# Second strips of three output projections by seven block products, with x spilled and reloaded around them

## The reference, cut to what matters

```
x = x + rmsnorm(mix, g[1])                 # mix   = [mixer result, 256 x 2048] @ w_out (2048 x 2048)
h = rmsnorm(x, g[2])
x = x + rmsnorm(cross_attention, g[3])     # ends in o @ wo (2048 x 2048)
h = rmsnorm(x, g[4])
x = x + rmsnorm(swiglu, g[5])
```

## Time and profile before

| what | us |
|---|---|
| median of 3 runs | 2858.02 (2857.41 to 2858.25) |
| span of the profiled execution | 2856.5 |
| TensorE busy | 2838.7 (99%) |
| VectorE busy | 2120.0 (74%) |
| ScalarE busy | 1546.4 (54%) |
| GpSimd busy | 49.2 (2%) |
| DMA | 582.54 MB, mean 204 GB/s |

### The profile page before, as it was taken

One profiled execution on the slowest core, in us unless ns is written; L12 is line 12 of the kernel. 1 busy time (PEld: TensorE's weight loads), 2 busy tenths in 40 slices (PEclk: granted clock), 3 DMA queues, 4 the chain that ended last, 5 costly groups with the idle time before them and its releaser, 6 DMA issues.

```text
span 2856.5 us, 31752 instructions
## 1 busy us (share of the span) xinstructions
PE 2838.7 (99%) x13038; PEld 2358.0 (83%) x13038; DVE 2120.0 (74%) x1454; ACT 1546.4 (54%) x1391; POOL 49.2 (2%) x102
## 2 busy tenths in 40 slices
PE   8999999999999999999999999999999999999998
PEld 7888888888888888888888888788888888888887
DVE  7888777669569988885556876569569888986444
ACT  6666555446346656664444665446446556655443
POOL 0000000000000000000000000000000000000000
PEclk9999999999999999999999999999999999999999
DMA  7674754655556556547555655655556566456552
GB/s 269 232 277 170 274 199 170 236 178 211 187 176 241 179 183 236 202 172 288 191 192 173 215 192 181 221 177 183 215 166 222 180 228 221 169 200 267 194 195 96
DMA packets 239233, 582.54 MB, mean 204 GB/s; under 512 B 8896, under 2 KB 8928, under 8 KB 223472
## 3 DMA queue, kind: packets, MB, share of 16 engines
q1 hardware_dynamic: 233792, 532.72, 52.6%
q0 software_dynamic: 4416, 37.29, 3.4%
q10 hardware_dynamic: 880, 10.49, 0.9%
HBM read 563.69 MB, written 16.78 MB: 203 GB/s over the span
## 4 chain that ended last, share of the span: by engine, by line
PE 97%; DMA 1%; DVE 1%; issue 1%; ACT 0%; SPq 0%; DVEq 0%; POOLq 0%; POOL 0%; ACTq 0%
PE ps L1842 95%; PE ps L1987 1%; PE ps L1973 1%; PE ps L2269 1%; DMA wide<-in_xattn_wk 0%; DMA memx<-in_mem 0%; ACT w_hi L585 0%; DVE w_lo L1143 0%; DVE w_lo L1137 0%; PE ps L2219 0%; ACT hx L691 0%; DVE act_lo L1282 0%; DVE hx L1354 0%; DVE xres L1829 0%; DVE hx L1343 0%
## 5 line engine op out<-in xcount | busy, mean ns | idle before, releaser
L1143 DVE TENSOR_TENSOR w_lo<-wide,w_hi 128x2048 fp32r<-128x2048 f32 x548 | 1244.2, 2288 | 449.6 <-ACT w_hi L585 446.5
L585 ACT ACTIVATE w_hi<-wide 128x2048 fp32r<-128x2048 f32 x548 | 1044.8, 1914 | 503.7 <-PE ps L1842 407.3
L1842 PE MATMUL ps<-w_hi,act_hi 128*128 128x512 f32 x3352 | 896.6, 391 | 1.0 <-ACT w_hi L598 1.0
L1842 PE MATMUL ps<-w_lo,act_hi 128*128 128x512 f32 x3352 | 891.2, 389 | 0.4 <-DVE w_lo L1143 0.4
L1842 PE MATMUL ps<-w_hi,act_lo 128*128 128x512 f32 x3352 | 890.8, 389 | 0.0
L1842 PEld LDWEIGHTS ps<-w_lo,act_hi 128*128 128x128 f32 x3352 | 629.2, 188 | 132.0 <-DVE w_lo L1143 1.2
L1842 PEld LDWEIGHTS ps<-w_hi,act_lo 128*128 128x128 f32 x3352 | 629.2, 188 | 131.2
L1842 PEld LDWEIGHTS ps<-w_hi,act_hi 128*128 128x128 f32 x3352 | 626.6, 188 | 132.0 <-issue 3.0
L1147 DVE TENSOR_TENSOR wide<-wide,wide 128x2048 f32<-128x2048 f32 x102 | 233.5, 2289 | 4.7
L1098 ACT ACTIVATE act_hi<-mid 128x256 fp32r<-128x256 f32 x80 | 33.4, 418 | 243.0 <-PE ps L1842 243.0
L585 ACT ACTIVATE w_hi<-w_sum 128x2048 fp32r<-128x2048 f32 x34 | 65.3, 1921 | 96.1 <-DVE w_sum L1147 88.6
(11 more groups left out here) (253 smaller groups left out, 1549.0 us busy)
## 6 DMA issues: line engine op xcount, KB each, us to landing
wide<-in_ffn_w_gate SPq DMA_DIRECT2D x88, 1024.0 KB, 8.1
wide<-in_ffn_w_up SPq DMA_DIRECT2D x88, 1024.0 KB, 7.4
wide<-in_ffn_w_down SPq DMA_DIRECT2D x88, 1024.0 KB, 4.8
wide<-in_odd_w_in SPq DMA_DIRECT2D x48, 1024.0 KB, 5.3
wide<-in_xattn_wk SPq DMA_DIRECT2D x32, 1024.0 KB, 7.6
wide<-in_xattn_wv SPq DMA_DIRECT2D x32, 1024.0 KB, 6.7
wide<-in_even_w_in SPq DMA_DIRECT2D x32, 1024.0 KB, 7.1
wide<-in_xattn_wq SPq DMA_DIRECT2D x32, 1024.0 KB, 5.2
```

The lines of the kernel that those rows point to most:

```text
L585: nc.scalar.activation(w_hi[:, c % W_SLOTS, :], src, ACT.Copy).then_inc(hi_done, 2)
L1143: nc.vector.tensor_tensor(w_lo[:, c % W_SLOTS, :], src, w_hi[:, c % W_SLOTS, :].bitcast(F32), ALU.subtract).then_inc(lo_done, 2)
L1842: return nc.tensor.matmul(dst, lhs, rhs, start=start, stop=stop, skip_group_check=loose)
```

## The change

The second strip of `x_out0`, `mix_out1` and `x_out1` becomes a summed strip. With it: token sums for these stages, laid in x's memory, so that x is spilled in the stage `xq` ahead of each `x_out` and reloaded in the second strip of each of the three; the last four chunks run by token tile, first all four for tile 0 and then for tile 1; two intermediate results are added into banks 3 and 2 by VectorE (`snaps_to_banks`), for which TensorE waits before chunk c+9; each token tile now has two last banks in the turn, not one. In the first strip's `rest8`, `x_second` moves from `before_7` to `before_6`, and the token sums take `before_7`.

```diff
-        stage(f"mix_out{l}", (False, False))
+        stage(f"mix_out{l}", (False, l > 0))
...
-        stage(f"x_out{l}", (False, False))
+        stage(f"x_out{l}", (False, True))
...
         def last_quad(st):
-            return [[(2, 3, (m0_done, st.a + 2))], [(3, 3, (w_used, st.c + 8 + W_SLOTS))]]
+            if st.g is None:
+                return [[(2, 3, (m0_done, st.a + 2))], [(3, 3, (w_used, st.c + 8 + W_SLOTS))]]
+            return [[(0, 2, (m0_done, st.a + 1)), (2, 3, (m0_done, st.a + 2))],
+                    [(1, 2, (w_used, st.c + 9 + W_SLOTS)), (3, 3, (w_used, st.c + SUMMED + W_SLOTS))]]
...
                 for s_kv in kv_out:
                     pool.wait_ge(s_kv, 16)
+                if l:
+                    reload_x("gla_qk", sums_used("mix_out1", 1))
                 turn_roots()
                 pool.wait_ge(h_done, 2 * NORMS.index(f"pre_x{l}") + 2)
                 pool.dma_start(kx[:].rearrange("p k t -> p (k t)"), kv_dram[l, 0]).then_inc(kv_in, 16)
+                spill_x(2 * (3 * l + 1))
                 pool.wait_ge(w_used, sums_used(f"xq{l}", 1))
                 pool.dma_start(vx[:].rearrange("p m n -> p (m n)"), kv_dram[l, 1]).then_inc(kv_in, 16)
                 pool.wait_ge(pv_done, 8 * (l + 1))
                 load_gain(norms[l, 3])
                 load_pre_gain(norms[l, 4])
+                reload_x(f"x_out{l}", sums_used(f"x_out{l}", 1))
                 turn_roots()
...
             def turn(st, last, nxt, summed=False):                      # ScalarE
                 early = len(last[1]) > 1
                 square_parts(0, last[0])
-                square_parts(1, last[1][:early])
-                split_halves(st, 0)
+                if summed:
+                    split_halves(st, 0)
+                    square_parts(1, last[1][:1])
+                else:
+                    square_parts(1, last[1][:early])
+                    split_halves(st, 0)
                 split_halves(st, 1)
...
                 lead(st1, lambda: (square_banks([(0, 0)], 0), square_banks([(1, 0)], 1)),
-                     lambda: (square_banks([(2, 1)], 0), square_banks([(3, 1)], 1)))
-                rest8(st1, before_7=lambda: (square_banks([(0, 2)], 0), square_banks([(1, 2)], 1)))
-                return turn(st_next, last_quad(st1), nxt)
+                     lambda: (square_banks([(2, 1)], 0), square_banks([(3, 1)], 1)),
+                     (lambda: token_hi(name)) if st1.g is not None else nothing)
+                if st1.g is None:
+                    rest8(st1, before_7=lambda: (square_banks([(0, 2)], 0), square_banks([(1, 2)], 1)))
+                else:
+                    rest11(st1, y[:, 0, 3 * NB:], y[:, 1, 3 * NB:])
+                return turn(st_next, last_quad(st1), nxt, st1.g is not None)
...
+            def snaps_to_banks(st, q_sb, p5_sb):                        # VectorE
+                dve.wait_ge(snap, 5 * st.g + 5)
+                nc.vector.tensor_tensor(ps[:, 3, :], ps[:, 3, :], p5_sb, ALU.add).then_inc(snaps_added, 1)
+                dve.wait_ge(w_used, st.c + 6 + W_SLOTS)
+                nc.vector.tensor_tensor(ps[:, 2, :], ps[:, 2, :], q_sb, ALU.add).then_inc(snaps_added, 1)
...
+                    if name[:5] == "x_out":
+                        dve.wait_ge(x_kept, kept_count(name))
...
+            def known_parts(m):
+                then(nc.vector.tensor_reduce(ssq[:, m:m + 1], ssq_part[:, m, 0:3], AX_X, ALU.add))
+                then(nc.vector.tensor_scalar(part[:, m:m + 1], ssq[:, m:m + 1], 1.0 / D, EPS, ALU.mult, ALU.add))
...
+                def first_bank(m):                                      # in VectorE's turn, after the
+                    squared()                                           # last h of tile 0 was begun for
+                    b, n, _ = last[m][0]                                # m = 0, and between split 0 and
+                    scaled_h(b, m, n)                                   # split 1 for m = 1
+                    free_bank(m, 0)
+                    if summed:
+                        known_parts(m)
...
                 rest_transposes(nxt, 1)
+                for ready in x_ready:
+                    dve.wait_ge(*ready)
                 x_update(0)
...
-                rest8(first, x_first, x_second)
-                lead(second, scale(0, 0), scale(0, 1))
-                rest8(second, before_7=scale(1, 0))
...
+                first_sums, other_sums = token_adds(name)
+                rest8(first, x_first, lambda: (first_sums(), other_sums()), x_second)
+                lead(second, scale(0, 0), scale(0, 1), lambda: token_lo(name))
+                rest11(second, before_9=lambda: snaps_to_banks(second, y[:, 0, 3 * NB:], y[:, 1, 3 * NB:]))
+                for b in range(4):
+                    dve.wait_ge(bank_free[b], second.u + 1)
+                return turn(st_next, last_quad(second), nxt, True, True, x_again_ready)
...
+                if at_end is not None:                                  # TensorE, strip11
+                    added = 2 * OUT_SUMMED.index(name)
+                    for m in range(MT):
+                        for j in range(7, SUMMED):
+                            q, k = (j - 7) // 2, 8 + 4 * ((j - 7) % 2)
+                            if m == 1 and j == SUMMED - 1:
+                                at_end(0)
+                            if m == 0 and j == 9:
+                                pe.wait_ge(snaps_added, added + 2)
+                            ins = product(c + j, tokens(k, m), 2 * q + m)
...
-                quad(second, 0)
-                quad_by_tile(second, 1, at_end=next_norm(nxt))
+                if second.g is None:
+                    quad(second, 0)
+                    quad_by_tile(second, 1, at_end=next_norm(nxt))
+                else:
+                    strip11(second, name, at_end=next_norm(nxt))
```

More of the change, by code:

```diff
@@ L116, in build, with kept_count, back_count @@
     POSTS = [f"{n}{l}" for l in range(LAYERS) for n in ("mix_out", "x_out", "down")]
-    SUM_STAGES = ["mk0", "sb_qk", "xq0", "gu0", "gla_qk", "xq1", "gu1"]
+    SUM_STAGES = ["mk0", "sb_qk", "xq0", "x_out0", "gu0", "gla_qk", "mix_out1", "xq1", "x_out1", "gu1"]
+    OUT_SUMMED = ["x_out0", "mix_out1", "x_out1"]
+    SPILLS = ["x_out0", "gu0", "gla_qk", "x_out1", "gu1"]
+    RELOADS = ["x_out0", "gu0", "gla_qk", "mix_out1", "x_out1", "gu1"]
+    def kept_count(name):
+        return 32 * (SPILLS.index(name) + 1)
+    def back_count(name):
+        return 16 * (RELOADS.index(name) + 1)
     def turn_counts(name, i):
@@ L794, in _, with turn @@
             xs_squared = [0]
-            def turn(st, last, nxt):
+            def turn(st, last, nxt, summed=False):
                 early = len(last[1]) > 1
                 square_parts(0, last[0])
-                square_parts(1, last[1][:early])
-                split_halves(st, 0)
+                if summed:
[4 more added lines that the diff above has]
+                    split_halves(st, 0)
                 split_halves(st, 1)
@@ L1384, in free_bank @@
                     scaled_y(b, m, n).then_inc(bank_free[b], 1)
+                def first_bank(m):
[5 more added lines that the diff above has]
+                        known_parts(m)
+                early = len(last[1]) > 1
                 for k, (b, n, _) in enumerate(last[0]):
+                    if summed and k == 0:
+                        first_bank(0)
+                        continue
                     squared()
@@ L1395, in turn @@
                 free_bank(0, len(last[0]) - 1)
[L1396 to L1400, removed]
+                if early and not summed:
+                    first_bank(1)
                 split(st, 0, (0, 1))
-                if not early:
+                if summed:
+                    first_bank(1)
+                if known:
                     split(st, 1, (0, 1))
                 rest_transposes(nxt, 0)
-                if early:
+                if not known:
                     split(st, 1, (0, 1))
@@ L1456, in x_second @@
                     both_gains()
-                rest8(first, x_first, x_second)
-                lead(second, scale(0, 0), scale(0, 1))
-                rest8(second, before_7=scale(1, 0))
[L1460 to L1463, removed]
-                    then(nc.vector.tensor_scalar(part[:, m:m + 1], ssq[:, m:m + 1], 1.0 / D, EPS, ALU.mult, ALU.add))
-                return turn(st_next, last_quad(second), nxt, True)
+                if second.g is None:
+                    rest8(first, x_first, x_second)
+                    lead(second, scale(0, 0), scale(0, 1))
+                    rest8(second, before_7=scale(1, 0))
+                    for m in range(MT):
+                        dve.wait_ge(bank_free[m], second.u + 2)
+                        dve.wait_ge(bank_free[2 + m], second.u + 1)
+                        known_parts(m)
+                    return turn(st_next, last_quad(second), nxt, True)
```

(2 more changed lines are left out.)

32 lines of the change are left out of this document (21 added, 11 removed).

## The result

| what | before | after |
|---|---|---|
| median time, us | 2857.72 (2857.4 to 2858.25, 4 runs) | 2873.05 (2872.92 to 2873.22, 4 runs) |
| span of the profiled execution, us | 2856.5 | 2871.4 |
| matmuls | 13038 | 13002 |
| longest wait of TensorE for ScalarE behind the start, us | 0.6 | 10.6 |

The changed kernel takes 1.0054 of the time before (95% interval 1.0042 to 1.0066), 15.3 us more. The prediction said 2872.3, in a range of 2863 to 2879, and gave "slower" 0.84.

A forecast was written before the change was run, and what follows sets the result against it. TensorE was taken to bound the kernel, busy 2838.7 of 2856.5 us. Forecast: 2858.0 - 8.2 (matmuls saved) + 20.8 (waits) + 1.7 (clock) = 2872.3 us, range 2863 to 2879.

The forecast's parts named there:

- The saving: Three summed strips: seven products stand for eight, 36 matmuls fewer at 0.2268 us, 8.2 us off TensorE's path.
- The waits on bank 2: Second product of each summed strip: TensorE waits 3.6 us in x_out0, 10.6 in mix_out1, 3.6 in x_out1.
- The first `snap`: Third product of each summed strip waits for ScalarE's copy of bank 0 to bank 1: 1.0 us more.
- The clock: Slow matmuls after the 10.6 us wait in mix_out1: 1.7 us net, with bounds of nothing and 5.2.
- the fourth rival: Clock stays low longer: slow matmuls after all three waits, over two products; 7.8 in place of 1.7, 2878.4 us; chance 0.07.
- At no cost: Rest of the strip, loads, turn, ScalarE's extra square and x's reload and spill: all taken as covered, costing nothing.
- the chunk c+9: VectorE's two additions of `snaps_to_banks` come some 16 us behind c+2's start, TensorE asks at 19: cover 3 us.
- the turns: `first_bank(1)` adds 1.6 us; transposes end at 9.9, rounded tile needed at 12.6; without cover up to 1.6 three times.
- the third rival: Late loads on top: x's reload delays c+8, 2.3 us a strip, 2879.2 us; chance 0.06.
- The first: Rival: bank 2 is free in time and only the saved products count, 2849.8 us; chance 0.06.
- The second: Rival: the waits in x_out shrink under the cover, that of mix_out1 stays, 2863.1 us; chance 0.08.
- the fifth: Rival: saved matmuls come back as waits on single products with about the same sum, within 0.2%; chance 0.03.

The follow-up runs named there:

- The last two kernels: Changed kernel with VectorE's work spread into its gaps and x's reload after the turn's first root: 2849.36 us; that with mix_out0 summed too: 2846.76 us.
- the wait of 2.30 us further up: In x_out0 of the changed kernel with VectorE's work spread into its idle stretches, reload of x still early: 2853.35 us.

## Why the prediction was right

**The saving.** 36 matmuls less, at the pace of the earlier trace rows 8.2 us. The last two kernels collect it in full (2.7 us a strip), so the price of the matmul was right.

**The waits on bank 2.** Said 3.6, 10.6 and 3.6, measured 3.48, 10.60 and 3.49. The chain of durations along VectorE's order, from the last split that still waited for ScalarE to the square, was out by 0.1 us in 37 in x_out0. It could be that exact because VectorE had no gap in it, so that only durations counted. The kernel with one more operation shows that this is the cause: the same length came out at TensorE. The kernel with bank 2 read early shows that it is the place and not the amount.

**The first `snap`.** I had 1.0 us in each strip. It is seen once, in x_out1 (0.47, and 0.77 over the pace in all). In the other two the slow second product covered it, which the text had allowed for mix_out1 and not for x_out0. Priced at the 0.77 of x_out1 in each strip, this term is 2.3, for which I had 3.0.

**The clock.** I took 1.7 net for mix_out1 and nothing for the waits of 3.6, with an upper bound of 5.2. Measured are 2.57 in x_out0 and 2.18 in mix_out1, `snap` included; net of the same 0.77 that is 1.80 and 1.41, 3.2 in all. This was the term mis-sized downwards, 1.7 for 3.2: a slow stretch came after one of the two shorter waits too. In x_out0 it ended with the first matmuls of the third product (1.22 for four, behind 2.08, 1.91 and 1.91), so it lasted a little over one product and not two, and it came after two waits and not three, so the fourth rival was wrong. Clock and `snap` together were 4.7 in the sum and are 5.5 in the trace: errors of opposite sign, and that the forecast of 2872.3 lies only 0.8 us from the measurement is in this part luck. The Trainium skill, "TensorE: Matmul & The Clock Gate", section "Why this matters for your kernels", has gaps above some 3 us as the danger. In the changed kernel the trace agrees in mix_out1 and x_out0 and not in x_out1, and the wait of 2.30 us further up shows a fall below that.

**At no cost.** The moves of x (the kernel with these alone is within 0.1% of the one before), the rest of the strip, the chunk c+9 and the turns: no wait of TensorE in any of them. In x_out0 of the changed kernel ScalarE waits 0.90 and 0.41 us for the loads of c+9 and c+10 without TensorE feeling it. Here the cover was thin: once the strip started on time, a late load of the third rival's kind was real, 2.3 and 1.1 us.

**The rivals.** The first, bank 2 free in time at 2849.8, was wrong for this order and right for another: 2849.36 with the order repaired and the reload moved. It needed what I had named, VectorE at least 3.6 and 10.6 us ahead: with its work spread into the gaps it reads bank 2 5.6 us sooner in x_out0 and 14.7 in mix_out1 (1891.55 against 1906.28), of which 1.9 are the stage's own earlier start. The second (waits in x_out vanish) and the fifth did not happen.

What stays open: why the clock falls in one x_out stage and not in the other. And why the runs of the kernel with the gains of mix_out1 earlier lie 7 us apart has no run of its own. Its reload is issued at 824.44, in the midst of the same loads, and ScalarE waits 3.58 us for one of them, but TensorE does not wait behind it in the profiled execution; that the reload spreads these runs too is an argument from the one case where the move was tried.

## What to carry to other kernels

A form that saves matmuls brings work to other engines, and what counts is not their share of busy time but the place of the one operation that frees the bank or slot that TensorE wants next. Write down the order of the in-order engine from its last real wait to that operation, add up the durations, and put short operations that release something ahead of long ones that don't. When such a wait is gone, look at the transfers next, and issue a reload that nobody waits for yet behind the loads that somebody does.

## What the hardware showed that was not expected

- The granted clock after a short wait is no fixed function of its length. After 3.5 us it fell in x_out0 and not in x_out1, in two profiles of the changed kernel; with mix_out1 plain it was the other way round. It fell after the one wait of 2.30 us, and after all of 4.7 (one), 5.9 (two), 10.6 (two) and 12.9 us (one). Nor does what it costs follow the wait: from the second product to the third there are 5.29 us behind 3.48 and 4.24 behind 5.87.
- The fall can come after the matmuls have begun again. Behind the wait of 2.30 us the four matmuls at 835.06 took 1.19 us, those behind them 1.57 and 2.07; the clock was 1.00 from 833 to 835, 0.87 from 835 to 837 and 0.52 from 837 to 840.
- A transfer of 2 MB by another queue, issued in the midst of 1 MB weight loads, moved the last of them by 6.2 us (ScalarE begins its split at 833.10 instead of 826.85), and the runs of that kernel spread over 8.4 us. With the transfer later they were within 0.8. The DMA share was full in both kernels in 825 to 830 (1.06 and 1.02), so the share alone does not tell which transfer is late.
